# Ninety single-precision products with the identity written as transposes of the tensor engine

## What is computed

```
def rms_norm(x, g):
    y = x * lax.rsqrt(jnp.mean(x * x, axis=-1, keepdims=True) + NORM_EPS)
    return y * g

for l in range(2):
    mod = (silu(c) @ ada_w[l] + ada_b[l]).reshape(B, 3, 3, D)      # the conditioning rows
    h = rms_norm(x, norm_g[l, 0]) * (1 + mod[:, 0, 1]) + mod[:, 0, 0]
    x = x + 0.5 * mod[:, 0, 2] * swiglu(h, ffn_w_in[l, 0], ffn_w_out[l, 0])
    h = ...                                                        # norm, scale, shift
    x = x + mod[:, 1, 2] * token_mix(h, ...)
    ...                                                            # second feed-forward part
# in token_mix, the gated delta rule:
beta = sigmoid(b_raw)                                              # 4 heads x 256 tokens
kb = k * beta[..., None]
o = rms_norm(chunk_gated_delta_rule(q, k, v, g, beta), norm_g) * silu(z)
```

## Time and profile before

| | |
|---|---|
| median of three runs | 2044.21 us |
| the three runs | 2035.01, 2044.21, 2048.25 us |
| the profiled execution's span | 2038.6 us |
| instructions | 45985 |
| mean granted TensorE clock | 0.973 of full speed |

### The profile page before, as it was taken

One profiled execution on the slowest core, in us unless ns is written; L12 is line 12 of the kernel. 1 busy time (PEld: TensorE's weight loads), 2 busy tenths in 40 slices (PEclk: granted clock), 3 DMA queues, 4 the chain that ended last, 5 costly groups with the idle time before them and its releaser, 6 DMA issues.

```text
span 2038.6 us, 45985 instructions
## 1 busy us (share of the span) xinstructions
PE 1928.1 (95%) x19510; PEld 1676.8 (82%) x19510; DVE 883.3 (43%) x2006; ACT 417.5 (20%) x1051; POOL 827.0 (41%) x858
## 2 busy tenths in 40 slices
PE   6999999989999999999998999999999898888898
PEld 3999988769999999998877999997877777744455
DVE  3577543444553377624354433125554444311112
ACT  1211032341110111103234111011443210110011
POOL 2888731006888687863100688920032200001110
PEclk9999999999999999999999999999998899899999
DMA  9789832404775499843341344543321111999995
GB/s 391 258 317 351 306 112 101 152 26 176 253 256 200 146 325 337 326 155 114 105 147 36 130 168 176 175 145 114 104 74 44 34 45 47 368 410 390 365 382 205
DMA packets 111360, 405.81 MB, mean 199 GB/s; under 512 B 13888, under 2 KB 14144, under 8 KB 110400
## 3 DMA queue, kind: packets, MB, share of 16 engines
q1 hardware_dynamic: 87408, 325.61, 43.5%
q10 hardware_dynamic: 19152, 71.05, 9.7%
q0 software_dynamic: 4608, 6.31, 0.9%
HBM read 445.91 MB, written 1.05 MB: 219 GB/s over the span
## 4 chain that ended last, share of the span: by engine, by line
PE 85%; DVE 5%; DMA 4%; issue 2%; ACT 2%; POOL 2%; SPq 0%; DVEq 0%; POOLq 0%; ACTq 0%
PE ps L867 27%; PE ps L912 14%; PE ps L1355 8%; PE ps L2054 4%; PE ps L3381 3%; PE ps L2128 3%; PE ps L3365 2%; PE ps L3407 2%; PE ps L2527 2%; DMA ring<-in_experts_down 2%; PE ps L3418 2%; DMA ring<-in_weights 1%; PE ps L1352 1%; PE ps L2179 1%; PE ps L2137 1%
## 5 line engine op out<-in xcount | busy, mean ns | idle before, releaser
L867 PE MATMUL ps<-sq,arena 128*128 128x128 f32 x2112 | 251.9, 276 | 0.0
L831 POOL TENSOR_TENSOR arena<-ring 128x512 f32<-128x512 f32 (+1 forms) x176 | 175.7, 998 | 171.2 <-PE ps L867 107.0
L867 PEld LDWEIGHTS ps<-sq,arena 128*128 128x128 f32 x2112 | 244.5, 193 | 0.1
L867 PE MATMUL ps<-h,ring 128*128 128x128 f32 x1408 | 178.6, 279 | 5.6 <-ACT h L653 3.1
L836 POOL TENSOR_TENSOR arena<-ring,arena 128x512 f32<-128x512 f32 (+1 forms) x176 | 176.9, 1005 | 13.8
L834 POOL TENSOR_TENSOR arena<-arena,ring 128x512 f32<-128x512 f32 (+1 forms) x176 | 178.5, 1014 | 0.0
L832 POOL TENSOR_TENSOR arena<-ring 128x512 f32<-128x512 f32 (+1 forms) x176 | 177.3, 1007 | 0.0
L867 PEld LDWEIGHTS ps<-h,ring 128*128 128x128 f32 x1408 | 167.9, 194 | 9.1 <-ACT h L653 4.7
L1355 PE MATMUL ps<-h,ring 128*128 128x256 f32 x768 | 173.8, 384 | 0.0
L912 PE MATMUL ps<-arena 128*128 128x128 f32 x1408 | 173.6, 275 | 0.0
L912 PEld LDWEIGHTS ps<-arena 128*128 128x128 f32 x1408 | 165.3, 192 | 0.0
(11 more groups left out here) (584 smaller groups left out, 3189.6 us busy)
## 6 DMA issues: line engine op xcount, KB each, us to landing
ring<-in_weights SPq DMA_DIRECT2D x427, 512.0 KB, 4.0
arena<-in_weights ACTq DMA_DIRECT2D x86, 512.0 KB, 5.2
arena<-in_experts_up SPq DMA_DIRECT2D x16, 2048.0 KB, 17.8
ring<-in_experts_up SPq DMA_DIRECT2D x16, 2048.0 KB, 20.1
cst<-in_weights ACTq DMA_DIRECT2D x42, 512.0 KB, 5.4
arena<-in_experts_down SPq DMA_DIRECT2D x8, 2048.0 KB, 16.9
ring<-in_experts_down SPq DMA_DIRECT2D x8, 2048.0 KB, 21.6
cst<-in_consts ACTq DMA_DIRECT2D x1, 1860.0 KB, 9.9
```

The source lines that it names most:

```text
L831: pool.tensor_tensor(to[:, 0], a21, a22, ALU.add).then_inc(S("sum_one"), 1)
L867: mm = pe.matmul(into, weight[:, k], moving[:, k], start=(k == 0), stop=(k == half - 1))
```

## The change

The change replaces `pe.matmul(out, data, ident, start=True, stop=True)` by `pe.transpose(out, data, ident)` at six places: the turns of the conditioning rows (L517, L542), the spreads of the norm roots (L693, L765), of beta (L1493) and of the delta rule's output roots (L1580). These are 90 calls: 4 and 36 turns, 4 and 14 norm roots, 16 columns of beta, 16 output roots. The transposes of the rows give all 128 (or 64) columns where the product gave 4 (or 2), so each round goes to a bank of its own and VectorE reads every 32nd column of it. No instruction is moved on any engine, no wait is added or taken away, and no transfer is touched; the order of all rows of all five engines is the same but for the sizes of the turned rows. The spreads whose output is 64 partitions wide (L1478 and three in the second block) and the warming products stay products.

```
@@ ada_front_pe @@
-            mm = pe.matmul(bank(4, 4, 4)[:, m], mod_rows[:, m * P:(m + 1) * P], ident[:, 0:P:32], start=True, stop=True)
+            mm = pe.transpose(bank(4, 4, P)[:, m], mod_rows[:, m * P:(m + 1) * P], ident)
@@ ada_turn_pe @@
-        for r, groups, _, rows in ada_rounds(call):
+        for r, groups, b, rows in ada_rounds(call):
             n = 32 * groups
             for m in range(4):
-                mm = pe.matmul(bank(7, 16, 4)[:, 4 * r + m, 0:groups], rows[0:n, m * P:(m + 1) * P], ident[0:n, 0:n:32],
-                               start=True, stop=True)
+                mm = pe.transpose(bank(b, 4, P)[:, m, 0:n], rows[0:n, m * P:(m + 1) * P], ident[0:n, 0:n])
@@ mod_dve @@
-            own_dve(dve.tensor_tensor(by_group(mod[:, 0:width]), bank(4, 4, 4).rearrange("p m g -> p g m"), by_group(bias), ALU.add))
+            own_dve(dve.tensor_tensor(by_group(mod[:, 0:width]), bank(4, 4, P)[:, :, 0:P:32].rearrange("p m g -> p g m"), by_group(bias), ALU.add))
...
-                own_dve(dve.tensor_tensor(by_group(mod[:, part]), bank(7, 16, 4)[:, 4 * r:4 * r + 4, 0:groups].rearrange("p m g -> p g m"),
+                own_dve(dve.tensor_tensor(by_group(mod[:, part]), bank(b, 4, P)[:, :, 0:32 * groups:32].rearrange("p m g -> p g m"),
@@ norm_pair_pe @@
-                mm = pe.matmul(bank(4 + which, TT, P)[:, t], rstd[:, at:at + 1].broadcast_to((P, P)), ident, start=True, stop=True)
+                mm = pe.transpose(bank(4 + which, TT, P)[:, t], rstd[:, at:at + 1].broadcast_to((P, P)), ident)
@@ spread_pe @@
-            mm = pe.matmul(ps[:, norm_bank(n), T + t * P:T + (t + 1) * P], rstd[:, t:t + 1].broadcast_to((P, P)), ident, start=True, stop=True)
+            mm = pe.transpose(ps[:, norm_bank(n), T + t * P:T + (t + 1) * P], rstd[:, t:t + 1].broadcast_to((P, P)), ident)
@@ decays @@
-                    mm = pe.matmul(bank(4 + c, 4, P)[:, hd], beta[:, c, hd:hd + 1].broadcast_to((P, P)), ident, start=True, stop=True)
+                    mm = pe.transpose(bank(4 + c, 4, P)[:, hd], beta[:, c, hd:hd + 1].broadcast_to((P, P)), ident)
@@ o_spread @@
-                    mm = pe.matmul(bank(hd // 2, 2, T)[:, hd % 2, c * P:(c + 1) * P], o_rn[:, at:at + 1].broadcast_to((P, P)), ident, start=True, stop=True)
+                    mm = pe.transpose(bank(hd // 2, 2, T)[:, hd % 2, c * P:(c + 1) * P], o_rn[:, at:at + 1].broadcast_to((P, P)), ident)
```

More of the change, by code:

```diff
@@ L588, in mod_dve @@
             by_group = lambda v: v.rearrange("p (g m) -> p g m", g=4)
-            own_dve(dve.tensor_tensor(by_group(mod[:, 0:width]), bank(4, 4, 4).rearrange("p m g -> p g m"), by_group(bias), ALU.add))
+            own_dve(dve.tensor_tensor(by_group(mod[:, 0:width]), bank(4, 4, P)[:, :, 0:P:32].rearrange("p m g -> p g m"), by_group(bias), ALU.add))
         else:
             dve.wait_ge(S("ada_sums"), call + 1)
-            for r, groups, _, _ in ada_rounds(call):
+            for r, groups, b, _ in ada_rounds(call):
                 part = slice(at + 16 * r, at + 16 * r + 4 * groups)
                 by_group = lambda v: v.rearrange("p (g m) -> p g m", m=4)
-                own_dve(dve.tensor_tensor(by_group(mod[:, part]), bank(7, 16, 4)[:, 4 * r:4 * r + 4, 0:groups].rearrange("p m g -> p g m"),
+                own_dve(dve.tensor_tensor(by_group(mod[:, part]), bank(b, 4, P)[:, :, 0:32 * groups:32].rearrange("p m g -> p g m"),
                                           by_group(bias[:, 16 * r:16 * r + 4 * groups]), ALU.add))
```

## The result

The changed kernel takes 2030.81 us in the median of 20 runs, the kernel before 2040.28 us in 20 runs beside them. The ratio is **0.9961, with an interval from 0.9945 to 0.9976**: by this ratio 8.0 us less, 5 to 11 (the two medians by themselves lie 9.5 us apart). That is clear of noise, and under 1%. The prediction was a saving of 9.1 us, a median of 2035, a range from 2024 to 2047, and a change of under 1% with a chance of 0.94.

The account below looks back on a forecast made before the run. The prediction took TensorE to bound the kernel over most of the span. Its terms, 3.9 + 1.8 + 1.8 + 0.9 + 0.5 + 0.2 = 9.1 us, came off the 2044.21 us median to give 2035 us, range 2024 to 2047.

Parts of the forecast that it names:

- Two pairs for a product, one for a transpose: At all changed calls a transpose saves one load-and-matmul pair of two: 0.114 us a spread, 0.108 a turn.
- What sets the pace: On TensorE the load of 128 weight columns, not the moving side, paces products and transposes; a transpose costs 0.109 us.
- The price of a turn: Turns of calls 1 to 4 (L542): each saves 0.108 us, 3.9 us for 36 calls.
- Norm terms: Norms 1, 2, 4, 5: VectorE waits for the spread, first products for h; 0.9 us together.
- The start: Norm 0 and first turns (L517) save nothing; the wait for GpSimd near 44 us grows about 0.7 us.
- VectorE's reads: VectorE's reads of every 32nd column were put at no extra cost; 1 us if each were a tenth dearer.
- Output roots, beta, calls 1 to 4, pair, norm 9: Savings counted: output roots 1.8 us, beta 1.8, turns of calls 1 to 4 3.9, norm pair 0.5, norm 9 0.2.
- The falling clock: TensorE's clock falls after thinned stretches at norms and mixers' ends; seven falls lose 11.8 us, giving 2047 us; chance 0.13.
- Hidden in part: In the mixers 16 beta columns and 8 turns of call 2 bring nothing (2.7 us): 2038 us; chance 0.12.
- no effect: Broadcast columns are transposed at the product's price and turns in two pairs: 2044 us; chance 0.05.
- A factor of four: Each transpose costs a quarter of the product; 82 calls save 13.5 us, giving 2031 us; chance 0.08.

Follow-up runs that it names:

- five_wide: Kernel before, each of the 90 products issued five times, turns as products with the whole identity as moving side; ratio 1.0374 to the kernel before.
- pace: Changed kernel plus groups of back-to-back transposes and products on the identity ahead of norm 4; transposes 0.108 us apart with 128 moving columns, 0.064 with 64.
- turns_only: Changed kernel with its 50 spreads put back to products, only the 40 turns staying transposes; ratio 0.9960 to the kernel before.
- five_transposes: Changed kernel with each of its 90 transposes issued five times in a row; ratio 1.0119 to the kernel before.
- five_products: Kernel before with each of the 90 products issued five times in a row, turns with 4 or 2 moving columns; ratio 1.0495 to the kernel before.

## Why the prediction was right, and where its working was not

- **Two pairs for a product, one for a transpose.** Right, to the instruction: 19420 matmuls, spacing 0.109, beta 1.04 us, the last turns 1.47 us, five_wide on the sum by pairs. Where a broadcast column is the stationary side, which no row of before showed, a transpose costs the same 0.109.
- **What sets the pace.** The prediction said that the load of 128 weight columns paces both. For products it does; for transposes pace shows that it doesn't. The number was right by luck: both take 0.11 us for 128 columns. For the eight turns of 64 rows the reason would have mattered, at 0.064 in place of 0.109 us 0.4 us in all, but the pieces of calls 1 and 3 show next to nothing of it (0.94 us each, where call 2, with 128 rows throughout, has 0.92).
- **The price of a turn.** It was put 0.006 us too low. In the row at 883.47 the second matmul starts 0.03 us behind the first and all others 0.11, so dividing by 23 gave 0.108 where the pairs are 0.112 apart. A turn saves 0.114 us and not 0.108 (1.37 / 12 in call 4), 0.2 us over the 36.
- **Norm terms.** Norms 1 and 4 gave 0.27 and 0.28 us (0.23 predicted). Norm 5 gave nothing and norm 2 0.20 us, of which 0.17 were the clock. The step that failed was to let "VectorE waits for the spread and the first products wait for h" decide for norms 2 and 5; behind them GpSimd's sums bind as behind norm 3. The fall of the clock at norm 2 in the trace of before had hidden that wait: with the clock full TensorE waits 0.99 us for the sums in turns_only and 1.24 us in the changed kernel, so the 0.2 us saved goes into the wait. Behind norm 5 it is a matter of 0.1 us. In the changed kernel the sums end at 1127.88 and the products that need them start at 1127.94, while the products ahead of them would have let them start at 1127.80 (1.78 us behind 1126.02, as before):

```profile
1126.02 1.95 PE L866 MATMUL ps<-h,ring 128*128 128x128 f32 x16
...
1126.60 1.28 POOL L835 TENSOR_TENSOR arena<-ring,arena 128x512 f32<-128x512 f32 x1
...
1127.94 1.16 PE L866 MATMUL ps<-h,arena 128*128 128x128 f32 x8
```

The rest of the 0.3 us is gone by the row behind (1129.11, and 1144.92 before).
- **The start.** The prediction's sign did not appear. The wait before 44 us is 2.68 us and not 0.7 longer than 3.20, since the clock is lower ahead of it in this execution (0.61 and 0.54 from 32 to 40 us, 0.96 and 0.61 before) and TensorE arrives later. The products behind the wait start 0.4 us sooner (44.48 for 44.87), but that came with a weight chunk: GpSimd's first sum, which waits for it, starts 0.4 us sooner (32.59 for 32.98). That the turns and norm 0 gave nothing is in keeping with this and not shown by itself.
- **VectorE's reads.** Nothing, as put: 0.17 us each in both traces.
- **Output roots, beta, calls 1 to 4, pair, norm 9.** Each within 0.1 us of its term.
- **The falling clock.** The clock does fall at the norms, but the change did not bring it on: at norms 1 to 5, the pair and the mixers' ends the changed kernel's trace has 1.00. The rival saw only thinner activity. The change also replaced a kind of work behind which the clock can fall while TensorE is busy, streams of 4 columns, by transposes; no trace has a fall at a transposed turn of calls 1 to 4. How much of the 8.0 us comes from this is open: turns_only has 4 us more than its pairs explain, the changed kernel as a whole has none beyond its sum.
- **Hidden in part, and no effect.** Out, by the table of pieces (call 2 0.92, beta 1.82 us) and the matmul counts. **A factor of four** is out by the spacing and by five_transposes.

## What to carry to other kernels

A single-precision product with the identity is two load-and-matmul pairs, a transpose one; count the matmuls of a line against its calls before pricing it. With 128 stationary columns a moving side of a few columns bought nothing in a product (0.11 us a pair for 4, 64 and 128), and it could cost the clock. Before pricing a fall of the clock or a shorter spread, look for what binds next behind it: behind norms 2 and 3 GpSimd's sums took both, behind norm 4 a fall cost 1.3 us in turns_only.

## What had not been expected of the hardware

- TensorE busy without a gap on products of 4 moving columns falls to its lower level (0.50 granted from 948 to 964 us in five_products), and pairs go from 0.11 us apart to about 0.2 (20 matmuls in 4 us). The same loads with 128 moving columns hold 1.00 (five_wide), but behind products of 64 rows with 64 moving columns it fell too (0.64 and 0.63 in five_wide, 0.65 in pace). Why these and not others is open.
- A single-precision transpose goes by its moving side: 0.109 us for 128 moving columns, 0.084 for 97, 0.064 for 64, with 128 stationary columns each time. A product's pair takes 0.11 us for 4, 64 or 128 moving columns, and 0.055 us with 64 stationary and 128 moving ones (L1478).
- 256 transposes in a row hold the full clock for 28 us.
